# The opening of a fused layer: the norms as two numbers a row, q from raw activations, and mem's chain moved to chunk 30

## What is computed

```python
def rms_norm(x, g):
    xf = x.astype(jnp.float32)
    y = xf * lax.rsqrt(jnp.mean(xf * xf, axis=-1, keepdims=True) + EPS)
    return (y * g.astype(jnp.float32)).astype(x.dtype)
...
    h = rms_norm(x, pre_g)
    proj = h @ w_in
    splits = [BRANCH_W * i for i in range(1, 8)]
    a_u, a_v, a_g, b_x, b_g, x_q, x_g, gate_logits = jnp.split(proj, splits, axis=-1)
    y_a = spatial_gating(a_u, a_v, sg_ln_g, sg_ln_b, sg_w, sg_b) * jax.nn.silu(a_g)
    y_b = s5_branch(b_x, a_re, a_im, log_dt, b_re, b_im, c_re, c_im, d, glu_w, glu_b) * jax.nn.silu(b_g)
    y_x = memory_cross_attention(x_q, rms_norm(mem, mem_g), xa_wk, xa_wv) * jax.nn.silu(x_g)
```

## Time and profile before

| what | value |
|---|---|
| median of 3 runs | 2066.32 us (2062.45 to 2068.18) |
| profiled execution | 2064.09 us |
| its span on the core | 2062.0 us |
| PE busy | 2005.4 us, 97% |
| DVE busy | 1571.2 us, 76% |
| ACT busy | 978.3 us, 47% |
| POOL busy | 410.8 us, 20% |
| mean granted clock of PE | 0.99 |

### The profile page before, as it was taken

How to read it: one execution, slowest core, us unless ns; L and a number is a source line. 1 busy time by engine, 2 the same in 40 slices (tenths; PEclk the granted TensorE clock), 3 DMA queues, 4 the chain that set the end, 5 groups by cost and what they waited for, 6 DMA issues and landing times.

```text
span 2062.0 us, 30943 instructions
## 1 busy us (share of the span) xinstructions
PE 2005.4 (97%) x12224; PEld 1749.3 (85%) x12224; DVE 1571.2 (76%) x2489; ACT 978.3 (47%) x1439; POOL 410.8 (20%) x293
## 2 busy tenths in 40 slices
PE   7899999999999999999999999999999999999997
PEld 6787888888878888888799987888888888888886
DVE  8766888888799986697899986777567657656765
ACT  5445444444444445557543346544344434434442
POOL 2400134333334320000287644000000000000000
PEclk9999999999999999999999999999999999999998
DMA  7554555444445455565456664555555555555553
GB/s 294 195 182 166 184 182 173 161 166 154 166 161 175 164 188 180 187 220 196 139 181 199 200 206 144 184 190 188 193 186 193 189 190 191 188 193 186 192 190 117
DMA packets 106704, 378.02 MB, mean 183 GB/s; under 512 B 11968, under 2 KB 15808, under 8 KB 106560
## 3 DMA queue, kind: packets, MB, share of 16 engines
q1 hardware_dynamic: 106560, 376.04, 54.2%
HBM read 373.01 MB, written 2.98 MB: 182 GB/s over the span
## 4 chain that ended last, share of the span: by engine, by line
PE 79%; DVE 14%; ACT 2%; issue 2%; DMA 1%; SPq 0%; DVEq 0%; ACTq 0%
PE bank L1777 44%; PE bank L1779 23%; DVE bank L1545 3%; DVE wl L1003 3%; PE bank L1767 1%; PE bank L1766 1%; PE bank L1768 1%; ACT wh L643 1%; PE bank L1782 1%; PE bank L1784 1%; PE bank L1783 1%; PE bank L1806 1%; DVE sq L1010 1%; DVE uT L1054 1%; DVE scr L1034 1%
## 5 line engine op out<-in xcount | busy, mean ns | idle before, releaser
L1003 DVE TENSOR_TENSOR wl<-raw,wh 128x1024 fp32r<-128x1024 f32 x593 | 739.3, 1250 | 348.0 <-ACT wh L643 346.3
L643 ACT ACTIVATE wh<-raw 128x1024 fp32r<-128x1024 f32 x680 | 712.2, 1055 | 536.6 <-PE bank L1779 395.1
L1777 PE MATMUL bank<-Hr,wh 128*128 128x512 f32 x2432 | 860.9, 398 | 8.4 <-DVE wl L1003 4.1
L1777 PE MATMUL bank<-Yr,wh 128*128 128x512 f32 x2176 | 767.1, 396 | 16.1 <-DVE wl L1003 12.3
L1779 PE MATMUL bank<-Hr,wl 128*128 128x256 f32 x2432 | 682.6, 281 | 0.0
L1779 PE MATMUL bank<-Yr,wl 128*128 128x256 f32 x2176 | 610.5, 281 | 0.0
L1777 PEld LDWEIGHTS bank<-Hr,wh 128*128 128x128 f32 x2432 | 457.9, 188 | 121.2 <-issue 7.1
L1777 PEld LDWEIGHTS bank<-Yr,wh 128*128 128x128 f32 x2176 | 408.9, 188 | 113.5 <-DVE wl L1003 11.3
L1779 PEld LDWEIGHTS bank<-Hr,wl 128*128 128x128 f32 x2432 | 461.2, 190 | 0.3
L1779 PEld LDWEIGHTS bank<-Yr,wl 128*128 128x128 f32 x2176 | 412.0, 189 | 0.2
L586 POOL TENSOR_TENSOR wl<-raw,wh 128x1024 fp32r<-128x1024 f32 x87 | 215.0, 2480 | 410.2 <-ACT wh L643 387.3
(11 more groups left out here) (321 smaller groups left out, 1759.9 us busy)
## 6 DMA issues: line engine op xcount, KB each, us to landing
raw<-in_w_up SPq DMA_DIRECT2D x128, 512.0 KB, 4.3
raw<-in_w_dn SPq DMA_DIRECT2D x128, 512.0 KB, 4.3
raw<-in_w_g SPq DMA_DIRECT2D x96, 512.0 KB, 3.2
raw<-in_w_p SPq DMA_DIRECT2D x80, 512.0 KB, 3.2
raw<-in_w_b SPq DMA_DIRECT2D x48, 512.0 KB, 3.2
raw<-in_w_out SPq DMA_DIRECT2D x32, 512.0 KB, 3.2
raw<-in_w_bx SPq DMA_DIRECT2D x16, 512.0 KB, 5.1
raw<-in_w_q SPq DMA_DIRECT2D x16, 512.0 KB, 3.5
```

What stands on the lines that cost most here:

```text
L643: e.activation(wh[:, c % WN, :], raw[:, c % RAW, :], ACT.Copy).then_inc(s_hi, 1)
L1003: e.tensor_tensor(wl[:, c % RAW, :], raw[:, c % RAW, :], wh[:, c % WN, :].bitcast(F32), ALU.subtract).then_inc(s_low_v, 1)
L1777: e.matmul(dst.rearrange("p (h t) -> p h t", h=2), lh, pair.both[:, :, k, :], start=first_part and kk == 0, stop=last_part and kk == 7, sk ...
```

## The change

- **Loads.** The first weight chunk is loaded ahead of x's second quarter, and the others are interleaved with x anew; the large load of constants goes behind chunk 6. ACT's and DVE's parts of chunks 2, 3 and 4 move along, so that chunk 4's high part stands ahead of the last quarter of x.
- **Norms in two numbers a row.** DVE folds x's squares to 4 tiles (mem's to 2). PE sums them with products that have 1 column (`stats`), so that mean squares stand as 128 rows by 2 columns. Epsilon, root and reciprocal work on those 2 columns (`norm_rows`). DVE spreads them on a diagonal (`across`, 128 x 256), PE multiplies by the matrix of 1/2048, and ACT copies the result, times 2048, into `r_x` (`norm_across`).
- **Places.** x's norm moves from chunk 5 to 9 and 10; the two folds to 6 and 7. The steps of `scaled` for x move from chunks 6 to 15 to 11 to 16, 18, 20, 22 and 24. bx results that ended before the norm wait and are multiplied at chunk 11.
- **q from raw activations.** q's chunks are multiplied with `hp0`, as bx's, and the result is multiplied by `r_x` on DVE (`times_norm`).
- **mem.** Its squares stay on 17 to 20; the three folds stand at 22, 24 and 26, its sums at 29, the broadcast at 30, the scaling at 31 to 40.

The core of the diff (declarations of semaphores and one moved wait for `s_hl` at k are left out):

```diff
@@ -200,9 +200,10 @@
-RX = 5
-MEM_SQ, MEM_R = 17, 23
-MEM_N = 26
+RX = 10
+X_N = (11, 12, 13, 14, 15, 16, 18, 20, 22, 24)
+MEM_SQ, MEM_R = 17, 30
+MEM_N = 31
@@ -401,6 +402,7 @@
+    rs_x, rs_mem = st[:, 0:2], st[:, 2:4]
@@ -531,15 +534,16 @@
+        chunk(0)
         e.dma_start(Xf[:, 4:8, :], a["xT"][:, 4:8, :]).then_inc(s_x[1], 16)
-        chunk(0)
         chunk(1)
+        chunk(2)
         e.dma_start(Xf[:, 8:12, :], a["xT"][:, 8:12, :]).then_inc(s_x[2], 16)
-        chunk(2)
+        chunk(3)
         e.dma_start(Xf[:, 12:16, :], a["xT"][:, 12:16, :]).then_inc(s_x[3], 16)
+        for c in range(4, RAW):
+            chunk(c)
         e.dma_start(cst[:, 16:NCONST], a["cst"][:, 16:NCONST]).then_inc(s_cst, 16)
-        for c in range(3, RAW):
-            chunk(c)
@@ -646,6 +650,11 @@
+        def norm_across(n, dst):
+
+            w.wait_ge(s_rb, n)
+            e.activation(dst, bank[7][:, 0:T], ACT.Copy, scale=2048.0).then_inc(s_rstd, 1)
+
@@ -664,7 +673,7 @@
-                w.wait_ge(s_hl, 8)
+                w.wait_ge(s_hl, 4)
@@ -915,39 +925,42 @@
-            if i < 3:
-                high(i)
-        for i in range(4):
-            e.activation(sq0[:, 4 * i:4 * i + 4, :], Xf[:, 4 * i:4 * i + 4, :], ACT.Square).then_inc(s_xq, 1)
-            if i == 1:
-                high(3)
-        w.wait_ge(s_cst, 16)
+            for c in ((0,), (1, 2), (3, 4), ())[i]:
+                high(c)
         for c in range(1, NC + 1):
-            if c == RX:
-                root(1, r_x)
+            if c in (1, 2):
+                for i in (2 * c - 2, 2 * c - 1):
+                    e.activation(sq0[:, 4 * i:4 * i + 4, :], Xf[:, 4 * i:4 * i + 4, :], ACT.Square).then_inc(s_xq, 1)
             if c in (end("gt", 1), LAST_PAD):
                 for j in ENDED[c]:
                     evac(j)
-            if c + 3 < NC and c + 3 not in HIGH_POST and c + 3 not in HIGH_LN and c not in (LN2 - 1, LN2):
+            if 4 < c + 3 < NC and c + 3 not in HIGH_POST and c + 3 not in HIGH_LN and c not in (LN2 - 1, LN2):
                 high(c + 3)
             if c not in (end("gt", 1), LAST_PAD):
                 for j in ENDED.get(c, ()):
                     evac(j)
-            if RX + 2 <= c < RX + 10:
-                u = 2 * (c - RX - 2)
+            if c == RX:
+                w.wait_ge(s_cst, 16)
+                norm_across(1, r_x)
+            if c == RX - 1:
+                root(1, rs_x)
+            if c - 1 in X_N[0:8]:
+                u = 2 * X_N.index(c - 1)
                 w.wait_ge(s_xn, u // 2 + 1)
                 e.activation(hp.hi[:, u:u + 2, :], Xf[:, u:u + 2, :], ACT.Copy).then_inc(s_hh, 1)
             if MEM_SQ <= c < MEM_SQ + 4:
                 i = c - MEM_SQ
                 w.wait_ge(s_mem[i], 16)
-                w.wait_ge(s_rstd, 1)
-                e.activation(sq0[:, 4 * i:4 * i + 4, :], Mf[:, 4 * i:4 * i + 4, :], ACT.Square).then_inc(s_mq, 1)
+                w.wait_ge(s_mean, 1)
+                e.activation(sq0[:, 4 * i:4 * i + 4, :], Mf[:, 4 * i:4 * i + 4, :], ACT.Square).then_inc(s_xq, 1)
+            if c == MEM_R - 1:
+                root(2, rs_mem)
             if c == MEM_R:
-                root(2, r_mem)
+                norm_across(2, r_mem)
             if MEM_N + 1 <= c < MEM_N + 9:
                 u = 2 * (c - MEM_N - 1)
                 w.wait_ge(s_mn, u // 2 + 1)
-                w.wait_ge(s_mm, end("bx", 7))
+                w.wait_ge(s_mm, end("q", 7))
@@ -1003,13 +1016,27 @@
-        def tree():
-            n = 16
-            while n > 2:
-                n //= 2
-                e.tensor_tensor(sq0[:, 0:n, :], sq0[:, 0:n, :], sq0[:, n:2 * n, :], ALU.add).then_inc(s_v, w.own())
+        def squares_folded(n):
+
+            w.wait_ge(s_xq, 4 * n)
+            e.tensor_tensor(sq0[:, 0:8, :], sq0[:, 0:8, :], sq0[:, 8:16, :], ALU.add).then_inc(s_v, w.own())
+            yield
+            w.wait_ge(s_v, w.n)
+            if n == 2:
+                e.tensor_tensor(sq0[:, 0:4, :], sq0[:, 0:4, :], sq0[:, 4:8, :], ALU.add).then_inc(s_v, w.own())
+                yield
                 w.wait_ge(s_v, w.n)
-            e.tensor_tensor(sq0[:, 0:1, :], sq0[:, 0:1, :], sq0[:, 1:2, :], ALU.add).then_inc(s_sum, 1)
+            h = 4 // n
+            e.tensor_tensor(sq0[:, 0:h, :], sq0[:, 0:h, :], sq0[:, h:2 * h, :], ALU.add).then_inc(s_sum, 1)
+
+        def norm_rows(n, v):
+            w.wait_ge(s_mean, n)
+            e.tensor_scalar(v, bank[7][:, 0:2], 1e-6, None, ALU.add).then_inc(s_eps, 1)
+            w.wait_ge(s_root, n)
+            e.reciprocal(v, v).then_inc(s_v, w.own())
+            w.wait_ge(s_v, w.n)
+            w.wait_ge(s_id, 1)
+            across(v, 0, s_xdg)
@@ -1032,6 +1059,11 @@
+
+        def times_norm(j):
+            w.wait_ge(s_comb, j.comb)
+            w.wait_ge(s_rstd, 1)
+            e.tensor_tensor(kept(j), kept(j), r_x, ALU.mult).then_inc(s_u, 1)
@@ -1049,13 +1081,13 @@
-                w.wait_ge(s_comb, j.comb)
-                w.wait_ge(s_rstd, 1)
-                e.tensor_tensor(uT[:, t, :], uT[:, t, :], r_x, ALU.mult).then_inc(s_u, 1)
+                if j.end > RX:
+                    times_norm(j)
             elif j.stage == "q":
                 w.wait_ge(s_half, j.half)
                 e.scalar_tensor_tensor(qT[:, t, :], bk[:, 0:T], 1.0 / 16, qT[:, t, :], ALU.mult,
                                        ALU.add).then_inc(s_comb, 1)
+                times_norm(j)
@@ -1623,28 +1655,32 @@
-            if i < 3:
-                low(i)
-        low(3)
-        w.wait_ge(s_xq, 4)
-        tree()
-        w.wait_ge(s_cst, 16)
+            for c in ((0,), (1, 2), (3,), ())[i]:
+                low(c)
+        x_folded, mem_folded = squares_folded(1), squares_folded(2)
         main_setup, main_scales = s5_setup(), s5_scales()
         for c in range(1, NC + 1):
             if c + 3 < NC and c not in (POST, LAST_PAD, LN2 - 1):
                 low(c + 3)
-            if c == RX:
-                rstd(1, r_x, 1e-6)
+            if c in (RX - 4, RX - 3):
+                next(x_folded, None)
             for j in ENDED.get(c, ()):
                 evac(j)
-            if RX < c <= RX + 10:
+            if c == RX - 1:
+                norm_rows(1, rs_x)
+            if c == RX:
+                w.wait_ge(s_cst, 16)
+            if c == RX + 1:
+                for t in range(8):
+                    if AT["bx", t].end <= RX:
+                        times_norm(AT["bx", t])
+            if c in X_N:
                 w.wait_ge(s_rstd, 1)
-                scaled(c - RX - 1, Xf, "pre", r_x, s_xn, s_hh, hp, s_hl)
-            if c == MEM_SQ + 4:
-                w.wait_ge(s_mq, 4)
-                tree()
-            if c == MEM_R:
-                rstd(2, r_mem, 1e-6)
+                scaled(X_N.index(c), Xf, "pre", r_x, s_xn, s_hh, hp, s_hl)
+            if c in (MEM_SQ + 5, MEM_SQ + 7, MEM_SQ + 9):
+                next(mem_folded, None)
+            if c == MEM_R - 1:
+                norm_rows(2, rs_mem)
@@ -1721,7 +1757,7 @@
-        ACTS = {"bx": (hp0, s_x0l, 1, 0), "q": (hp, s_hl, 2, 0), "av": (hp, s_hl, 2, 0), "k": (mp, s_ml, 2, 0),
+        ACTS = {"bx": (hp0, s_x0l, 1, 0), "q": (hp0, s_x0l, 1, 0), "av": (hp, s_hl, 2, 0), "k": (mp, s_ml, 2, 0),
@@ -1827,6 +1863,18 @@
+        def mean_squares(n):
+            w.wait_ge(s_ones, 1)
+            w.wait_ge(s_sum, n)
+            w.wait_ge(s_rstd, n - 1)
+            for t in range(4 // n):
+                ins = stats(sq0[:, t, :], 0, first_part=t == 0)
+            ins.then_inc(s_mean, 1)
+
+        def norm_across(n):
+            w.wait_ge(s_xdg, n)
+            e.matmul(bank[7][:, 0:T], ones, dg[:, 0:2, :], start=True, stop=True).then_inc(s_rb, 1)
+
@@ -1925,17 +1973,14 @@
-            if c == RX:
-                w.wait_ge(s_sum, 1)
-                mean(sq0[:, 0, :])
-            if c == MEM_R:
-                w.wait_ge(s_sum, 2)
-                w.wait_ge(s_eps, 1)
-                mean(sq0[:, 0, :])
+            if c in (RX - 1, MEM_R - 1):
+                mean_squares(1 if c == RX - 1 else 2)
+            if c in (RX, MEM_R):
+                norm_across(1 if c == RX else 2)
             if c in (BIAS + 1, BIAS + 3):
                 h = (c - BIAS) // 2
                 w.wait_ge(s_tril, 1)
-                w.wait_ge(s_eps, 2)
+                w.wait_ge(s_rstd, 2)
```

More of the change, by code:

```diff
@@ L439, in _build @@
     s_sum, s_mean, s_eps, s_root, s_rstd = sem("s_sum"), sem("s_mean"), sem("s_eps"), sem("s_root"), sem("s_rstd")
+    s_xdg, s_rb = sem("s_xdg"), sem("s_rb")
     s_ones, s_id = sem("s_ones"), sem("s_id")
@@ L442, in _build @@
     s_xn, s_hh, s_hl = sem("s_xn"), sem("s_hh"), sem("s_hl")
-    s_mq, s_mn, s_mh, s_ml = sem("s_mq"), sem("s_mn"), sem("s_mh"), sem("s_ml")
+    s_mn, s_mh, s_ml = sem("s_mn"), sem("s_mh"), sem("s_ml")
     s_u = sem("s_u")
@@ L675, in evac @@
             elif j.stage == "k":
+                w.wait_ge(s_hl, 8)
                 half(j, KT[:, t, :])
```

## The result

The changed kernel took 2069.62 us in the median (2064.81 to 2073.43, 20 runs), the kernel before in the same measurement 2064.64 (2061.67 to 2069.47, 20 runs). The ratio is 1.0018, with a 95% interval of 1.0011 to 1.0025: 3.7 us slower (2.3 to 5.2). Forecast were 2066.0 us and "no change" within 0.3%. That bound holds, but it was wide: the prediction took 0.3% as about what a measurement can tell, and 20 runs of each kernel told 0.07%. The sum of +0.2 to +1.3 us is too small. The profiled execution took 2070.0 us with a span of 2068.3.

What follows compares the result with a forecast made beforehand. PE, busy 97% of the span, was taken as the bound, so only its idle time, slow clock and added work count. An opening gain of 0 to 1.1 us less 1.3 for bias rows gave 2066 us, range 2062 to 2070.

Steps and rivals of the forecast that it cites:

- The sum of +0.2 to +1.3 us: Whole kernel: a gain of 0 to 1.1 us in the opening, less 1.3 for the bias rows, against the profiled 2064.09.
- The walk to chunk 31: Opening up to chunk 30: 13.8 to 14.9 us lost, less 0.9 for the start, against 14.0 before; gain 0 to 1.1.
- Start: First weight chunk loaded ahead of x's second quarter: ACT, DVE and PE come 0.9 us earlier.
- Norm of x: Chunks 9 and 10: 0.9 us wait for the second fold, 0.5 for the diagonal, 2.5 of PE work (sums 1.8, broadcast 0.7).
- Ring: ACT's and DVE's parts waiting in turn, high part 21 to 23: 7.7 us for PE's 5.55; PE waits 2.7, chunks 23 to 25.
- Weight chunk 27: PE idles 3.7 us before it, for mem's first fold and POOL's two low parts on DVE; the clock probably falls, 3.0 us.
- Norm of mem: Two sums 0.9 us and the broadcast 0.7, where the mean took 0.7; counted as 1.6 us lost.
- the term of the bias rows: mem's scaling slides onto the bias rows on DVE: PE's wait there grows by 1.3 to 1.4 us, to 2.1.
- Hr: DVE's low parts of the normed x; PE's 4.1 us wait for them and the clock fall behind it were to go.
- Lost before, up to chunk 30: 14.0: Kernel before, 25 chunks from 15.69 to 99.10 us: 83.4 us taken where 69.4 would do, 14.0 lost.
- the faster one: Rival, chance 0.22: POOL takes its turn later, waits of chunks 23 to 27 and the clock fall go; gain 7.1, 2059.2 us.
- The slower one: Rival, chance 0.10: clock stays at half or falls again around chunk 27; 3.0 and 1.9 us more, 2072.5 us.

Runs made afterwards that it cites:

- e3: The changed kernel with the low parts of chunks 26, 28 and 30 on DVE instead of POOL; ratio to the kernel before 0.9984 (0.9975 to 0.9993).
- e4: The kernel before with mem's scaling on turns 31 to 40 instead of 26 to 35, nothing else; ratio 1.001 (1.0001 to 1.0019).
- e2: The changed kernel with mem's three folds on turns 24, 26 and 27 instead of 22, 24 and 26; ratio to the kernel before 1.0015 (1.0006 to 1.0024).
- e5: The kernel before with q from raw activations and mem's scaling on turns 31 to 40; ratio 1.0001 (0.9991 to 1.0012).
- e1: The changed kernel with DVE's bias rows ahead of mem's scaling; ratio to the kernel before 0.9998 (0.9989 to 1.0007).
- e8: The changed kernel with bias rows ahead of mem's scaling and low parts of chunks 26, 28, 30 on DVE; ratio to the kernel before 0.9982 (0.9972 to 0.9992).
- e9: The changed kernel with bias rows ahead of mem's scaling and low parts of chunks 22 to 30 on DVE; ratio to the kernel before 0.9962, median 2057.72 us.
- e11: The kernel before with only the change's order of loads at the start; ratio 0.9999 (0.9991 to 1.0008).

## Why the prediction was wrong

**The walk to chunk 31 came out right, in part by luck.** It gave a gain of 0 to 1.1 us; the first trace shows 0.6, the means of three traces 0.2 of loss at chunk 39. Its terms, by the first trace:
- Start: 0.9 forecast, 0.75 measured at chunk 1 (1.1 between the means of three).
- Norm of x: 3.9 forecast, 2.5 measured (chunks 9 to 11 took 8.0 us for 5.5). The sums were right: 16 rows at 0.12 us each, 1.9 against 1.8; the Trainium skill (TensorE: Matmul & The Clock Gate, Back-to-back issue gap) gives its 81 ns for 128 columns; taken for these sums of 1 column, as the prediction did, the estimate is 1.3, and here the trace differs and decides. The wait of 0.9 ahead of them wasn't there, though 0.8 was in the third trace. The row, of 30 to 110 us:

```profile
L1858 PE MATMUL bank<-ones,sq 128*128 128x1 f32 x24 | 2.9, 246 | 0.0
```

- Ring: 7.7 us forecast; the high parts of 21, 23 and 25 began at 69.27, 76.82 and 83.40, 7.55 and 6.6 apart. PE waited 0.8 us in two waits, and by the SyncE rows the 24th to 26th chunks took 1.7 us too long (3.44, 3.45 and 3.08 for 2.77), where 2.7 were forecast.
- Weight chunk 27: a wait of 5.2 instead of 3.7, since POOL got three low parts in, not two, and it began at 91.6, not 93.5. The clock fell behind it as forecast, for 2.7 us of loss.
- Norm of mem: 1.4 instead of 1.6, from the distances of the SyncE rows of chunks 29 to 31.

Errors of -1.4, -1.0 and +1.5 mostly cancelled. One was not in the walk at all: the first chunks took 2.83 us each, not 2.77 (14.94 to 37.56 for eight; why stays open).

**The step that failed is the term of the bias rows.** The prediction priced it as "1.3 to 1.4", with "Nothing covers them": the wait was right to 0.1 us (2.18, forecast 2.1), but the term held no fall of the clock behind it. It had charged such a fall to every longer wait (Hr, chunk 27) and none here, though in the trace of before a fall followed the wait of 4.05 and none the 0.79, which leaves a wait of 2.2 open between them. A fall costs 1.5 us more. It came in three of the seven traces with a bias wait of 2.18 (one of the change, e3, e4; not in e2 and e5), and in none of the ten with 0.8. The 40th chunk took 4.7 us in those ten, 6.1 in four of the seven and 7.6 in three. So the term is 1.4 or 2.9 us, 2.0 in the mean. Three pairs of kernels differ in this alone. Taking the term away gave back 4.1 us of time (e1 against the change, uncertain by 2.4) and 0.4 (e8 against e3, by 2.8); adding it to the kernel before cost 2.1 (e4, by 1.9). At chunk 60 it is 2.8, 3.5 and 2.8. The three times together, weighted by their intervals, make some 2.3 us, uncertain by 1.3: they show a loss, but by themselves can't tell 2.0 from the forecast's 1.3. The traces do, at the 40th chunk.

**The base failed too, and in the means it is the larger error.** The term "Lost before, up to chunk 30: 14.0" was read from one trace of before, 1.2 us slower in the opening than the mean of three. The first trace of the change happens to be late too, by 1.4 us at chunk 60 against its own mean, so the two first traces side by side don't show this. By means, the opening costs 2.1 us up to chunk 60, inside the 0.2 to 1.3 of the sum plus those 1.2; with the bias term at 2.0 the sum would be 2.1 to 3.2. Measured are 3.7 (2.3 to 5.2).

**The 1.6 us between 2.1 and 3.7 are not settled**: they lie within the interval. More frequent falls of the clock in the timed runs than in the traces of the opening would be one explanation, and the record of the timed runs goes with it: the mean granted clock was 0.9896 over the 20 runs of the change and 0.9906 over 81 runs of the kernel before (beside the experiments, on three chips). As an estimate from these and the two levels of 0.5 and 1, the change had some 4.3 us more at half speed, which loses 2.1 us (uncertain by 1.5). Where in the kernel they lie, no timed run shows.

**The rivals.** The ring was 7.55 and 6.6 us, not under 6, so the faster one didn't come. The slower one asked for PE to idle over 5 us between chunks 27 and 30 and so for 3.0 us more of slow clock; the wait alone was 5.2, but one fall of 6.8 us followed, already in the sum, and the loss came behind it.

**What stays open.** Why the kernels with the change and its loads have slower padded and shifted transfers (the second padded write took 5.2 us against 4.4, the last shifted read 4.6 against 3.9) and why the timed runs don't show those 3 us. The two falls of the clock at 1,236 to 1,250 us are not its mark: e4, with 75.0 us from 380 to 400, has two as well, from 1235.6 and 1245.8.

## What to carry to other kernels

A wait of the engine that bounds the kernel has two prices: its own length, and that of the clock if it falls behind it. Give each wait of one's sum both, with a chance for the second, and don't price a wait that grows from 0.8 to 2.2 us by the difference alone.

Where VectorE is late and a helper on GpSimd blocks it, try taking work from the helper: five low parts moved onto a DVE that was late already (e9 against e1) made the kernel 7.4 us faster (uncertain by 3), since each of POOL's cost a blocked DVE instruction up to 2.4 us and saved DVE 1.2 of work.

Before a difference of a few us is worked out from one trace, take two more of the same kernel: these lay 2.5 us apart in the first 200 us.

## What the hardware showed that was not expected

- POOL's ready low part gets in ahead of DVE's next instruction though DVE's are queued back to back: at 92.81, with the fold running from 91.18 to 93.46, the low part of 27 began its 3.35 us at 93.38 and had its port only when POOL was done at 95.66. So in this trace the helper got its turn between two DVE instructions.
- Whether the clock falls behind a given wait is not fixed by the kernel: behind the same 2.18 us it fell once in three traces; behind a wait for Hr of 3.2 us it didn't fall in two traces (one of before, e11) and did for 3.4 us in e4; at the 5.1 to 5.2 us of weight chunk 27 it fell for 6.8, 6.8 and 3.4 us, once already during the wait. A short wait is no surety either: in the third trace of the change a wait of 0.8 us and the sums of x's norm stood ahead of a fall of 3.4 us at 39.9, and the 10th chunk took 7.10 us instead of 4.81.
